# Decoder trunk with mixture of experts: an expert's rows picked by selection matmuls inside the expert loop, and six weight slots outside the ring in place of four

## What is computed

```python
def routed_experts(xf, expert_ids, combine, w_eg, w_eu, w_ed):   # xf (288, 1024), 2 experts a token, 32 experts
    ...
    rows = jnp.zeros((n_blocks * MOE_ROW_BLOCK, d), xf.dtype).at[dest].set(xf[order // k])   # sorted by expert
    def expert_block(args):
        xb, e = args
        hdn = jax.nn.silu(xb @ w_eg[e]) * (xb @ w_eu[e])     # 1024 -> 256, twice
        return hdn @ w_ed[e]                                 # 256 -> 1024
    ...
    return jnp.einsum('nkd,nk->nd', y_slots, combine.astype(y_slots.dtype))
```

## Time and profile before

| | us |
|---|---|
| median of 3 runs (lowest, highest) | 1150.87 (1149.61, 1157.13) |
| the profiled execution | 1153.77 |
| its span, first to last instruction | 1152.0 |
| PE busy | 991.5 (86%) |
| ACT busy | 465.6 (40%) |
| DVE busy | 386.1 (34%) |
| granted clock of PE, mean | 0.951 |

### The profile page before, as it was taken

How to read it: one execution, slowest core, us unless ns; L and a number is a source line. 1 busy time by engine, 2 the same in 40 slices (tenths; PEclk the granted TensorE clock), 3 DMA queues, 4 the chain that set the end, 5 groups by cost and what they waited for, 6 DMA issues and landing times.

```text
span 1152.0 us, 22124 instructions
## 1 busy us (share of the span) xinstructions
PE 991.5 (86%) x7680; PEld 636.3 (55%) x7681; DVE 386.1 (34%) x1075; ACT 465.6 (40%) x825; POOL 83.7 (7%) x163
## 2 busy tenths in 40 slices
PE   4899999899799899777779999999996989977775
PEld 2567677477575444333356767747775534433333
DVE  1128622222441233222242582231327023322224
ACT  2325564300234455444443456441014445544443
POOL 1112000000300000000002200000012000000000
PEclk9889998989988899999989999898997999999998
DMA  9894324993553889999996332299630288999991
GB/s 384 306 397 146 110 75 137 423 420 140 195 206 115 357 352 421 422 422 421 422 419 226 140 117 73 88 354 419 259 113 35 85 360 339 423 422 421 422 422 67
DMA packets 65422, 319.03 MB, mean 277 GB/s; under 512 B 6051, under 2 KB 27875, under 8 KB 28227
## 3 DMA queue, kind: packets, MB, share of 16 engines
q1 hardware_dynamic: 63408, 315.06, 68.7%
q10 hardware_dynamic: 1810, 2.51, 0.6%
q0 software_dynamic: 128, 0.40, 0.1%
HBM read 315.44 MB, written 2.51 MB: 276 GB/s over the span
## 4 chain that ended last, share of the span: by engine, by line
PE 62%; DMA 20%; DVE 9%; ACT 5%; issue 3%; SPq 1%; POOLq 0%; POOL 0%; DVEq 0%; PEldq 0%; ACTq 0%
DMA ring<-wstream 20%; PE ps L566 19%; PE ps L1000 7%; PE ps L643 7%; PE ps L940 4%; PE ps L977 3%; PE ps L990 3%; PE ps L1009 3%; PE ps L599 3%; PE ps L980 2%; PE ps L817 2%; PE ps L709 1%; DVE work L1331 1%; ACT work L1164 1%; DVE top L1330 1%
## 5 line engine op out<-in xcount | busy, mean ns | idle before, releaser
L1000 PE MATMUL ps<-ring,work 128*32 128x512 f32 x976 | 123.0, 619 | 53.3 <-DMA ring<-wstream 51.7
L566 PE MATMUL ps<-h,ring 128*128 128x288 f32 x512 | 134.9, 418 | 0.7 <-ACT work L1094 0.7
L566 PE MATMUL ps<-work,ring 128*128 128x288 f32 x512 | 131.6, 416 | 2.9 <-DVE work L1421 2.9
L566 PEld LDWEIGHTS ps<-work,ring 128*128 128x128 f32 x512 | 97.8, 194 | 30.0 <-issue 3.7
L566 PEld LDWEIGHTS ps<-h,ring 128*128 128x128 f32 x512 | 97.4, 195 | 29.9 <-issue 4.1
L643 PE MATMUL ps<-h,ring 128*128 128x288 f32 x416 | 106.5, 417 | 8.7 <-ACT h L1108 6.3
L1220 ACT ACT_TABLE_LOAD x64 | 82.1, 1283 | 58.1 <-issue 58.1
L643 PEld LDWEIGHTS ps<-h,ring 128*128 128x128 f32 x416 | 80.4, 195 | 33.1 <-issue 10.9
L1220 ACT ACTIVATE work<-ps 128x512 f32<-128x512 f32 x64 | 38.2, 598 | 142.3 <-PE ps L1000 142.3
L1567 DVE SCALAR_TENSOR_TENSOR h<-work 128x288 f32<-128x288 f32 x128 | 60.6, 514 | 105.0 <-issue 105.0
L1000 PEld LDWEIGHTS ps<-ring,work 128*32 128x32 f32 x976 | 26.8, 112 | 122.5 <-issue 119.9
(11 more groups left out here) (251 smaller groups left out, 1111.4 us busy)
## 6 DMA issues: line engine op xcount, KB each, us to landing
ring<-wstream SPq DMA_DIRECT2D x280, 1024.0 KB, 17.2
work<-wstream SPq DMA_DIRECT2D x8, 1024.0 KB, 20.2
work<-pages SPq DMA_DIRECT2D x32, 192.0 KB, 3.5
work<-pages SPq DMA_DIRECT2D x32, 128.0 KB, 2.2
cs<-consts SPq DMA_DIRECT2D x1, 1218.0 KB, 8.3
x<-x_in SPq DMA_DIRECT2D x1, 1152.0 KB, 5.1
out_y<-h ACTq DMA_DIRECT2D x2, 576.0 KB, 2.8
out_vp<-v ACTq DMA_DIRECT2D x2, 256.0 KB, 3.3
```

The source lines that it names most:

```text
L566: last = mm(out, w[:, (k0 + k) * stride:(k0 + k) * stride + 128], rhs(k), start=(k == 0), stop=(k == n - 1))
L1000: last = mm(pgu[32 * c:32 * c + 32, :], xs[:, k, :], ws[k // 4][:, c * 512:(c + 1) * 512], start=(k < 4), stop=(k >= 4), skip_group_check= ...
```

## The change

- The 16 jobs `x{k}.{hf}`, the job `rows` and `xsort` go. In their place PE takes each block's rows in the loop: `take_rows` (12 matmuls of 256 columns with 96 x 32 selection columns, into `px`, the former `pgut`), ACT copies them (`keep_rows`), PE turns them (`turn_rows`, 2 transposes) and ACT copies that into `xs` (`stage_rows`). The rows of the next block are taken while the present one is in work. POOL copies only the 96 x 3 x 32 selection of a block. The folded sums move into the second half of `py`, so folding now waits for `y_kept` too.
- Jobs `bc0` to `bc3` are made straight from `dest`, 3 matmuls each. DVE's seven steps that count blocks for `table` go to POOL. The second half of `sel` is made after the weights of the tokens.
- One Silu stands before the loop on ACT.
- `EXTRA` is 6 (pairs 12 to 17, experts 4 and 5 whole); the sixth is loaded once the last output projection is done. `EARLY` is 7, so 24 experts stay in the hardware loop and one is left behind it.

```diff
-EXTRA = 4
+EXTRA = 6
-EARLY, ROUND = 6, RING // 3
+EARLY, ROUND = 7, RING // 3
...
+                        g.wait_ge(rows_taken, n + l + 1)
+                        nc.gpsimd.tensor_copy(sel_block, sel[0:TB, :, bass.ds(at, BLK)]).then_inc(sel_staged, 1)
...
-                for i, (k, hf) in enumerate(GATHERS):
...
-                    ps = job(f"x{k}.{hf}")
...
                     for tb in range(3):
-                        last = mm(ps[:, 0:T], hrow[0:TB, tb, k * 128:(k + 1) * 128], sel[0:TB, tb, hf * T:(hf + 1) * T],
-                                  start=(tb == 0), stop=(tb == 2))
-                    filled(last, f"x{k}.{hf}")
+                        for c in range(4):
+                            last = mm(px[32 * c:32 * c + 32, 0:256], picks[:, tb, :],
+                                      hrow[0:TB, tb, c * 256:(c + 1) * 256], start=(tb == 0), stop=(tb == 2), skip_group_check=True)
+                    last.then_inc(rows_taken, 1)
+                def turn_rows():
+                    for i in range(2):
+                        last = nc.tensor.transpose(px[:, 256 + i * 128:256 + (i + 1) * 128], xrow[:, i * 128:(i + 1) * 128], ident)
+                    last.then_inc(rows_turned, 1)
...
+                take_rows(sel[0:TB, :, 0:BLK])
+                pe.wait_ge(rows_kept, pe.snap(seen, min_val=0, max_val=200) + l + 1)
+                turn_rows()
...
                 def turn_and_combine(n, last_block=False):
                     pe.wait_ge(gu_kept, n + 1)
+                    pe.wait_ge(y_kept, n + 1)
                     for i in range(4):
+                        last = mm(pgt[:, i * BLK:(i + 1) * BLK], gu[:, i * 128:(i + 1) * 128], fold[:, :], start=True, stop=True)
                     last.then_inc(gut_done, 1)
+                    pe.wait_ge(rows_kept, n + l + 2)
+                    if last_block:
+                        pe.sem_inc(rows_turned, 1)
+                    else:
+                        turn_rows()
                     combine(n)
...
+                    if ahead is not None:
+                        take_next()          # waits sel_staged, then take_rows(sel_block); after y_done and w_free
...
+                    act(xrow, px[:, 0:256], ACT.Copy).then_inc(rows_kept, 1)
...
+                    act(xs.rearrange("p (c i) s -> p i c s", i=2), px[:, 256:512].rearrange("p (i c s) -> p i c s", i=2, c=4),
+                        ACT.Copy).then_inc(x_staged, 1)
...
+                act(sg, sg, ACT.Silu).then_inc(silu_set, 1)
```

More of the change, by code:

```diff
@@ L114, in plan @@
     jobs += ["rank"] + [f"h{n}" for n in TURNS]
-    for i, (k, hf) in enumerate(GATHERS):
[L116 to L120, removed]
+    if l + 1 < DEPTH:
+        jobs += ["next_t"]
     jobs += [f"bc{i}" for i in range(4)]
@@ L496, in _ @@
                 xmix.wait(g, l)
-                step(padded_x, nc.gpsimd.memset(xsort[:, :, SLOTS:SLOTP], 0.0))
+                step(padded_x, nc.gpsimd.memset(sel[:, :, SLOTS:SLOTP], 0.0))
                 logits.wait(g, l)
@@ L924, in _, with take_rows @@
                     next_modulation(range(NEXT_EARLY, KD))
[L926 to L934, removed]
[L935 to L942 removed]
+                def take_rows(picks):
+                    for tb in range(3):
+                        for c in range(4):
[6 more added lines that the diff above has]
+                    last.then_inc(rows_turned, 1)
+                route.wait(pe, l, R_SEL0)
+                padded_x.wait(pe, l)
+                for n in TURNS:
+                    banks.wait_drained(pe, l, f"h{n}")
+                take_rows(sel[0:TB, :, 0:BLK])
+                hold(pe, seen)
+                pe.wait_ge(rows_kept, pe.snap(seen, min_val=0, max_val=200) + l + 1)
+                turn_rows()
+                if l + 1 < DEPTH:
+                    turn_modulation("next", "next_t")
                 for i in range(4):
@@ L946, in _ @@
                     if i == 0:
-                        route.wait(pe, l)
-                    filled(mm(ps[:, 0:T], cs[0:4, C_ONE:C_ONE + 128], rows4[0:4, i, :], start=True, stop=True), f"bc{i}")
+                        route.wait(pe, l, R_WTS)
+                    for tb in range(3):
+                        last = mm(ps[:, tb * TB:(tb + 1) * TB], bc(dest[0:TB, 7 + i, tb:tb + 1], [TB, 128]), ident[0:TB, 0:TB],
+                                  start=True, stop=True)
+                    filled(last, f"bc{i}")
                 zbanks = [banks.psum[b] for b in range(NBANK)] + [pzs]
@@ L1518, in _ @@
                                                         sel[0:TB, tb, part], ALU.is_equal, ALU.add))
[L1519 to L1527, removed]
+                select_rows(0)
+                assert route.n == R_SEL0, route.n
                 rexp.wait(d, l, 1)
@@ L1542, in _ @@
                 r(V.tensor_tensor(own, own, bc(cnt[:, 1, :].unsqueeze(2), shape), ALU.add))
[L1543 to L1547, removed]
-                banks.done(ins, l, "rows")
-                banks.wait_drained(d, l, "rows")
-                xtmp4.wait_so_far(d, l)
-                r(V.memset(comb, 0.0))
                 assert route.n == ROUTE, route.n
@@ L1557, in _ @@
                     banks.wait_drained(d, l, f"bc{i}")
+                tabled.wait(d, l)
                 hold(d, seen)
```

136 lines of the change are left out of this document (87 added, 49 removed).

## The result

The changed kernel takes 1229.89 us (median of 4 runs, 1223.33 to 1247.33) against 1152.12 for the kernel before, run beside it: 1.065 times as long, 95% interval 1.0586 to 1.0714. The run of 1247.33 was in a slower state and is left out of the ratio. I forecast 1168 and a range up to 1200. The sign was right, the size was not. The profiled execution has a span of 1221.6 us, 69.6 more than before's 1152.0.

The account below looks back on a forecast made before the run. PE, then DMA, was taken to bound the loop, and PE alone after the change. Per layer 27.9 us more in the loop, less 19.7 and 18.8 ahead of it, gave +17.3: 1171.1 profiled, 1168 median, range 1138 to 1200.

Parts of the forecast that it names:

- The sign: Whole kernel: slower, 1168 us forecast; chance 0.55 of slower by over 1%, 0.17 of faster by over 1%.
- What bounds the kernel, and where DMA stops bounding it: Expert loop: now 5.75 us an expert by PE, then 7.44 by DMA; after the change DMA no longer ends last anywhere.
- Ahead of the loop: From the gathers to the first `up`: a gain, 19.7 us sooner in layer 0 and 18.8 in layer 1.
- In the loop: PE's pace per expert: 5.75 plus `take_rows` 1.28, `turn_rows` 0.22 and waits 0.10 makes 7.35 us, between 7.2 and 7.9.
- The price of a step: `take_rows` in the loop: one side-by-side step of 256 columns is 0.43 us, three steps 1.28.
- the upper bound: `take_rows` in the loop: at most 1.58 us, from `down`'s 1.05 busy x 12/8.
- Table loads and slots: ACT's table loads in the loop and the two more slots: nothing gained from either.
- Rival E: New chain in the loop: a wait is missed, 0.2 us an expert, +12, so 1180 us; forecast with E 0.36.
- The early experts: First experts of each layer: code 1.4 times as long scales the losses of 13.3 and 12.3 us to 18.6 and 17.2.
- Rival C: First experts: code arrival sets the pace, 30 us lost a layer with the half clock, so 1192 us; chance 0.14.
- Rival B: First experts: longer passes let code arrive in time, early loss goes, so 1132 us; 0.17 together with a lower pass time.
- Rival D: Hardware loop: four experts' longer code is fetched again each pass, +91 to +130, so 1240 to 1300 us; chance 0.08.

Follow-up runs that it names:

- experiment 9: The changed kernel without the skipped branch, with 4 of the 12 `take_rows` matmuls in the loop: 1105.84 us, ratio 0.9597.
- experiments 7 and 8: The changed kernel without the skipped branch: with `EXTRA` 4 and `EARLY` 6, 1146.89 us; without the Silu ahead of the loop, 1141.59 us.
- experiment 3: The kernel before with 29 further matmuls in the branch that is never taken: 1191.15 us, ratio 1.0323.
- experiments 4 and 5: The changed kernel with never-run matmuls ahead of layer 0's expert loop: 32 of them 1189.47 us, 16 of them 1182.32 us.
- experiments 1 to 6: Changed kernel (1148.97 us) and kernel before (1136.21) without skipped branch; kernel before with longer branch (1191.15); changed kernel with 32, 16, 64 never-run matmuls ahead (1189.47, 1182.32, 1259.81).

## Why the prediction was wrong, point by point

- **What bounds the kernel, and where DMA stops bounding it: right.** DMA is never waited for in the changed kernel's loop.
- **Ahead of the loop: right.** 21.7 and 18.4 us sooner where 19.7 and 18.8 were worked out: 1.6 us too little in all. (Layer 1's terms as I listed them add up to 8.1 and not 7.8, so to 18.5 sooner.)
- **In the loop: the term was sized a little low.** 7.47 us, not 7.35: `take_rows` is 1.43 (timeline) to 1.50 (chain) from its start to the fold's, not 1.28. The price of a step, 0.43, holds (experiment 9), but the group's first step takes 0.64; the upper bound, 1.58 from `down`, held this. `turn_rows` 0.25 (0.22 worked out), the waits are met. 62 x 0.12 makes 7.4 us.
- **Table loads and slots: right** at nothing (experiments 7 and 8). Rival E fell: nothing was missed.
- **The early experts: right mechanism, too small.** 15.9 + 27.8 = 43.7 us lost while the loop's code runs for the first time; the sum had 18.6 + 17.2 = 35.8. The factor was the wrong tool. I scaled the loss with the code (1.4), but experiment 3 lengthens an expert's code about as much and adds 37 us. I also scaled the whole loss, and part of it is not code: 5.1 + 3.9 us stay in the kernel before without its branches, 2.1 + 2.7 in the changed one. The part that hangs on code goes from 16.6 to 38.9 us, 2.3 times for 1.4 times the code. It would do so if the loss were what an expert's work doesn't cover of a packet's arrival; that is a reading, not shown. Rival C, 30 us a layer, was the better picture for layer 1. Rival B had the sign the wrong way round: slower passes did not give the code time enough.
- **Rival D came true in part, and that is the failed step.** I reckoned that the hardware loop's code would stay, gave its refetch a chance of 0.08 and put it at nothing in the sum. It stayed in layer 1 and was fetched again in two turns of layer 0: 37.2 us by the starts of `up`, 40 to 48 by the medians with the loop moved, and nine packets of code in each of the two turns and none in the turns around them. The page of the Trainium skill that I leaned on ("Runtime: NRT & Kernel Launch", Instruction fetch mechanics: 128 KiB for PE, blocks of 16 KiB) fits a loop of six packets staying, as it does in layer 1 and with the loop moved; it doesn't tell why the same loop is refetched at two other places. Its section also speaks of a window of two blocks beyond which a taken branch has to fetch; by that the jump back over six packets would cost a fetch in every turn, and the turns without a packet disagree. And it calls the crossing into the next block mostly hidden. The runs here disagree: the code of the branches alone costs 16 to 18 us in the kernel before, where nothing is fetched again.

The terms together: +17.3 predicted, +7.4 for the pace, +7.9 for the early experts, -1.6 for the first `up`, +37.2 for the turns fetched again: +68.2, and the span grew by 69.6. Without the turns fetched again the kernel takes 1182 or 1189 (experiments 4 and 5), inside the range: two terms were off in size, one was left out of the sum. These two lie 14 and 21 us above the 1168 that I forecast, so the sum was low without the refetch too.

What isn't settled: which place makes a loop be fetched again, and which turns. Why layer 1's loop, with the same code, was spared is open too. What is settled: the pauses are PE waiting for code, they hang on the length and the place of code that is never run (experiments 1 to 6), and the change itself, freed of it, is 12.8 us slower than the kernel before freed of it.

## What to carry to other kernels

When "issue" pieces stand in the chain in the middle of a group whose inputs are there, count the code, dead branches included, and compare the packets of the instruction queue with the program's length: more packets than code means that a loop is fetched again, and the packets by window say in which turns. Moving work from ahead of a loop into it shortens the start, but in a loop bound by DMA the slots come free later, and in one bound by the engine it is paid once per pass; here both gave back all that was won. A case that never occurs in practice can be kept in a loop of its own behind one jump. Where the jump stands decides whether it pays: 0.6% faster with the jump ahead of the loop, nothing won with it behind.

## What the runs showed of the hardware

- A taken jump over code that isn't held costs 3.5 to 3.7 us ahead of the loop, at a DMA share of 0.02 to 0.05, and behind it lengthens the way to the next step by 6.4 and 7.3 us. The jumped-over code doesn't arrive: 46 packets, where the 42 of the kernel without branches and a second loop with them, twice 13, would make 68. That agrees with the Trainium skill ("Runtime: NRT & Kernel Launch", Instruction fetch mechanics): a taken branch to code outside what is held has to wait for its fetch. The short skipped branches behind `up` and `down` do arrive: 13 packets in the kernel before.
- 64 never-executed matmuls ahead of a loop made the kernel 30 us slower (1259.8 against 1229.9), 16 made it 48 us faster (1182.3).
- A turn of a loop of six packets, when fetched again, brought nine packets (changed kernel, 459.4 to 506.8 and 536.6 to 586.4 us), and none came in the turns between.
- PE paused for 4.41 us in code that ran for the first time while the DMA share was 0.02 (experiment 3).
